# Attention rows by pairs, long beside short, and results stored two rows at a time, in a hybrid pooling and stick-breaking trunk

## The reference

```
h = rms_norm(x) ; proj = h @ w_in
u_pool, z_pool, q, k, v, z_attn, gate_logits = split(proj)
y_pool = multiscale_pool(u_pool) * silu(z_pool)
# 8 heads of 64: strictly causal, no softmax
beta  = sigmoid(q.k / 8)
A[t,s] = beta[t,s] * prod_{s<j<t} (1 - beta[t,j])
y_attn = (A @ v) * silu(z_attn)
gates = sigmoid(gate_logits + b_gate)
merged = gates0 * (y_pool @ w_pool_up) + gates1 * (y_attn @ w_attn_up)
out = rms_norm(x + merged @ w_out)
```

## Time and profile before

| what | us |
|---|---|
| median of 3 runs | 1617.39 (1616.48 to 1621.03) |
| profiled execution, its own time | 1613.6 |
| its span, first to last instruction | 1611.6 |
| TensorE matmuls busy | 1562.7 (97%) |
| VectorE busy | 1237.0 (77%) |
| GpSimd busy | 974.6 (60%) |
| ScalarE busy | 775.5 (48%) |
| mean granted TensorE clock | 0.996 |

### The profile page before, as it was taken

The page is one execution under the profiler, slowest core; times in us unless marked ns, Lnnn a source line. Parts: engine busy times, 40 slices in busy tenths (PEclk is TensorE's granted clock), DMA queues, the critical chain, the costliest instruction groups (busy, mean ns, idle before and its releaser), DMA issues. The chain is left out here.

```text
span 1611.6 us, 24736 instructions
## 1 busy us (share of the span) xinstructions
PE 1562.7 (97%) x7934; PEld 1301.4 (81%) x7934; DVE 1237.0 (77%) x1662; ACT 775.5 (48%) x1492; POOL 974.6 (60%) x697
## 2 busy tenths in 40 slices
PE   7999999999999999999999999999999999999997
PEld 6887888788888887888877888888888787778886
DVE  6744524773889889998989978889888656677987
ACT  4412222223566666666666666666666411222342
POOL 3521102421679878887778887789876233446764
PEclk9999999999999999999999999999999999999999
DMA  7633335755434243353594432433423587764552
GB/s 251 230 126 127 137 105 183 236 165 174 118 121 113 78 114 105 105 135 97 180 317 166 143 100 83 115 99 115 118 72 114 188 271 226 245 195 153 188 187 107
DMA packets 163936, 245.78 MB, mean 153 GB/s; under 512 B 47697, under 2 KB 80977, under 8 KB 163810
## 3 DMA queue, kind: packets, MB, share of 16 engines
q1 hardware_dynamic: 163810, 244.20, 48.2%
HBM read 158.15 MB, written 85.99 MB: 151 GB/s over the span
## 5 line engine op out<-in xcount | busy, mean ns | idle before, releaser
L1576 DVE TENSOR_TENSOR_SCAN left<-keep,left 128x512 f32<-128x512 f32 x192 | 296.9, 1546 | 32.0 <-issue 19.9
L1403 PE MATMUL psum<-hT,ring 128*128 128x512 f32 x644 | 264.3, 410 | 4.5 <-DVE sum_d L1612 2.4
L1643 POOL TENSOR_TENSOR ring<-raw,ring 128x512 fp32r<-128x512 f32 x138 | 231.1, 1675 | 55.2 <-ACT ring L1483 40.2
L1407 PE MATMUL psum<-hT,ring 128*128 128x512 f32 x644 | 262.8, 408 | 0.0
L1405 PE MATMUL psum<-hT,ring 128*128 128x512 f32 x644 | 262.4, 407 | 0.0
L1489 ACT ACTIVATE keep<-psum 128x512 f32<-128x512 f32 (+3 forms) x320 | 170.5, 533 | 177.5 <-PE psum L1429 175.6
L1496 ACT ACTIVATE wt<-psum 128x512 fp32r<-128x512 f32 (+3 forms) x320 | 170.9, 534 | 110.1 <-PE psum L1437 107.2
L1449 PEld LDWEIGHTS psum<-wt,vm 128*128 128x128 f32 x1088 | 170.6, 188 | 32.7 <-issue 7.0
L1582 DVE TENSOR_TENSOR wt<-psum,wt 128x512 fp32r<-128x512 f32 (+3 forms) x320 | 189.7, 593 | 7.8 <-ACT wt L1496 5.2
L1449 PE MATMUL psum<-wt,vm 128*128 128x256 f32 x1088 | 181.6, 281 | 5.1 <-DVE row_sum L1591 4.3
L1437 PE MATMUL psum<-ident,left 128*128 128x128 f32 x1088 | 170.9, 272 | 1.4 <-DVE wt L1582 1.2
(11 more groups left out here) (217 smaller groups left out, 3387.4 us busy)
## 6 DMA issues: line engine op xcount, KB each, us to landing
raw<-in_w_strips SPq DMA_DIRECT2D x92, 256.0 KB, 3.9
qm<-qk_scratch SPq DMA_DIRECT2D x128, 128.0 KB, 4.2
gate<-gate_scratch SPq DMA_DIRECT2D x64, 256.0 KB, 4.5
hT<-form_scratch SPq DMA_DIRECT2D x28, 512.0 KB, 8.3
xt<-in_x SPq DMA_DIRECT2D x16, 512.0 KB, 4.9
xT<-in_x_T SPq DMA_DIRECT2D x16, 512.0 KB, 3.8
qk_scratch<-staging SPq DMA_DIRECT2D x32, 256.0 KB, 2.6
qk_scratch<-store_lo SPq DMA_DIRECT2D x32, 256.0 KB, 3.4
```

The lines of the kernel that those rows point to most:

```text
L1403: pe.matmul(o, hi, m_hi, start=k == 0, stop=False)
L1407: last = pe.matmul(o, lo, m_hi, start=False, stop=k == HK - 1)
L1576: dve.tensor_tensor_scan(left[:, n % LN, span][:, ::-1], k, k, carry, ALU.mult, ALU.bypass).then_inc(scanned, 1)
L1643: pool.tensor_tensor(out_, a, b, op).then_inc(s, 1)
```

## The change

Rows are taken by pairs in the order of `QUERY_ORDER` = 7, 0, 6, 5, 2, 4, 3, 1 in every pass: rows 15, 14, 1, 0, 13, 12, 11, 10, 5, 4, 9, 8, 7, 6, 3, 2. Items, query units and the steps of all loads follow from this order; the planner is the same and is applied to the new list. A y_out buffer now holds 256 columns, two rows, and each pair of rows is stored by itself; the waits for the buffers, the count awaited ahead of the last stage's attention values (now up to the store of pair 6 in the last pass) and the last store follow. The rest of the kernel is unchanged.

```diff
--- before.py
+++ after.py
@@ -157,7 +157,7 @@
 
         for u in range(2):
             self.load_k(sp, 0, u, 0, NC - 1 - u)
-            self.load_q(sp, 0, u, 0, TT // 2 - 1 - u)
+            self.load_q(sp, 0, u, 0, QUERY_ORDER[u])
         for u in range(2, NC):
             self.load_k(sp, 0, u, 0, NC - 1 - u)
 
@@ -999,11 +999,15 @@
             pe.wait_ge(lo_done, STRIPS + 1)
             pe.wait_ge(staged_lo, qk_order[STRIPS - 1, 0] + 1)
             strip_product(pe, psum[:, 0, :], w_hi[:, 0, :, :], w_lo[:, 0, :, :], hT, 1)
+QUERY_ORDER = (7, 0, 6, 5, 2, 4, 3, 1)
+
+
 def attention_items():
 
 
+    rows = [i for r in QUERY_ORDER for i in (2 * r + 1, 2 * r)]
     return [(e, i, c, (i % 4 + 1) * P if c == i // 4 else CH, c == i // 4, c == 0)
-            for e in range(2) for i in reversed(range(TT)) for c in reversed(range(i // 4 + 1))]
+            for e in range(2) for i in rows for c in reversed(range(i // 4 + 1))]
 
 
 def stage3(nc, sem, psum, sb, sb_raw, ring_at, ident, bcol, v_ends, hT, w_hi, w_lo, w_strips, mix_t, mix_d, yp_d, za_d,
@@ -1129,7 +1133,7 @@
 
     KN, VN, QN = HeadLoads.KN, HeadLoads.VN, HeadLoads.QN
     kv_units = [(e, c) for e in range(2) for c in reversed(range(NC))]
-    q_units = [(e, r) for e in range(2) for r in reversed(range(TT // 2))]
+    q_units = [(e, r) for e in range(2) for r in QUERY_ORDER]
     NK, NQ = len(kv_units), len(q_units)
 
     def key_items(u):
@@ -1155,7 +1159,7 @@
 
     def query_unit(n):
         e, i = item(n)[0:2]
-        return n // NI * NQ + TT // 2 * (e + 1) - 1 - i // 2
+        return n // NI * NQ + q_units.index((e, i // 2))
 
     def at(steps, s):
 
@@ -1183,7 +1187,7 @@
     wt = sb("wt", [P, WN, 4, 2, P], F32R)
     half_sum = sb("half_sum", [P, 2 * P])
     row_sum = sb("row_sum", [P, 2, 2 * P])
-    y_out = sb("y_out", [P, 2, CH])
+    y_out = sb("y_out", [P, 2, 2 * P])
     floor = sb("floor", [P, CH])
     raws = [{b: sb_raw(f"raw{i}_{b}", [P, HK, P]) for b in (A11, A12, S3, A22)} for i in range(2)]
     second = sb("second", [P, HK, P])
@@ -1234,7 +1238,8 @@
         g, o, a, c = result_out(k)
         sp.dma_start(gate_d[strip_of(g, a) - S_G, :, c * CH:(c + 1) * CH], sums[tile_index(k)]
                      ).then_inc(sum_stored[tile_index(k)], DMA)
-        sp.dma_start(at_d[PAIRS - 1, HD:P, 0:CH], y_out[HD:P, 1, :]).then_inc(y_stored[1], DMA)
+        last = 2 * P * QUERY_ORDER[-1]
+        sp.dma_start(at_d[PAIRS - 1, HD:P, last:last + 2 * P], y_out[HD:P, 1, :]).then_inc(y_stored[1], DMA)
 
     before_in_all = (4 * len(WINDOWS) + 2 * 4 * 2 * PAIRS) // 2 * DMA
     END = ALL + 10
@@ -1299,9 +1304,9 @@
 
             def store_y(n):
                 e, i = item(n)[0:2]
-                u = row_of(n) // 4
+                u = row_of(n) // 2
                 hold(y_done, row_of(n) + 1)
-                sp.dma_start(at_d[n // NI, e * HD:(e + 1) * HD, i * P:i * P + CH],
+                sp.dma_start(at_d[n // NI, e * HD:(e + 1) * HD, i * P:(i + 2) * P],
                              y_out[e * HD:(e + 1) * HD, u % 2, :]).then_inc(y_stored[u % 2], DMA)
 
             def open_stage4(s):
@@ -1317,7 +1322,7 @@
                     opening.load_z(sp, 1, tok)
                     for i in range(opening.EARLY):
                         opening.load_piece(sp, i)
-                    sp.wait_ge(y_stored[0], (PAIRS * 4 - 1) * DMA)
+                    sp.wait_ge(y_stored[0], (PAIRS * TT // 2 - 3 + QUERY_ORDER.index(6) // 2) * DMA)
                     opening.load_y(sp, 1, tok)
 
             for s in range(-2, END):
@@ -1351,7 +1356,7 @@
                     if s == RESULT[k] + 1:
                         store_result(k)
                 for n in LAST[:-1]:
-                    if item(n)[1] % 4 == 0 and s == n + AV_LAG + 4:
+                    if item(n)[1] % 2 == 0 and s == n + AV_LAG + 4:
                         store_y(n)
 
         @block.tensor
@@ -1677,11 +1682,11 @@
             def finish_row(n):
                 e, i, row = item(n)[0], item(n)[1], row_of(n)
                 mine = slice(e * HD, e * HD + HD)
-                u = row // 4
+                u = row // 2
                 pool.wait_ge(row_done, row + 1)
-                if i % 4 == 3:
+                if i % 2 == 1:
                     wait(pool, y_stored[u % 2], u // 2, DMA)
-                step(y_out[mine, u % 2, i % 4 * P:i % 4 * P + P], row_sum[mine, row % 2, 0:P],
+                step(y_out[mine, u % 2, i % 2 * P:i % 2 * P + P], row_sum[mine, row % 2, 0:P],
                      row_sum[mine, row % 2, P:2 * P], ALU.add, y_done, row + 1)
 
             def value_diff(u):
@@ -1961,7 +1966,7 @@
                     for s, count in zip(sum_stored, SUM_STORES):
                         sp.wait_ge(s, count * DMA)
                     for s in y_stored:
-                        sp.wait_ge(s, PAIRS * 4 * DMA)
+                        sp.wait_ge(s, PAIRS * TT // 2 * DMA)
                 if m == 0 and b == 1 and c + 1 < NC:
                     sp.wait_ge(up_done, at_up(c, 1, 0))
                     opening.load_y(sp, 0, tokens(c + 1))
```

## The result

The changed kernel took 1656.27 us, the median of 5 runs (1654.46 to 1658.34), against 1617.37 us for the kernel before on the same chip (5 runs, 1614.49 to 1621.03). The ratio is 1.0251, 95% interval 1.0233 to 1.027: 38.9 us slower. The forecast was slower, 1631.0, with a range to 1645, so the sign was right and the size was not. The profiled execution took 1655.26 us, its span is 1653.3 (before 1611.6), its mean granted clock 0.985 (before 0.996).

A forecast was written before the change was run, and what follows sets the result against it. TensorE, busy 842.0 of 856 us in the attention stage, was taken as the bound. The terms 16.9 + 3.6 + 1.0 + 1.0 - 4.3 - 4.6 = +13.6 us, put on 1617.39, gave 1631.0; range 1619 to 1645.

The forecast's parts named there:

- three stalls for the value part: Starts of passes 2, 3 and 4: TensorE waits for GpSimd's late low value part, 16.9 us in sum; forecast's mechanism, 76%.
- clock behind them: After the three stalls TensorE runs at half clock for a while: +3.6 us, bounds 0 and 5.1.
- passes 5 to 8, value part: Starts of passes 5 to 8: value part possibly late, 1.0 us at the fifth and 1.0 for the other three.
- row sums: Pass ends: rows end less crowded, so TensorE's three waits for a row's sum go, -4.3 us.
- query load: Into pass 5: the first query load goes out earlier, saving its wait, -3.0 us, and -1.6 for the clock.
- key loads: Last key units get fewer steps between load and use; cost put at 0, hidden behind the items between.
- VectorE's slack: Attention stage: VectorE busy 753.6 of 856 us, taken to cover the two one-item rows behind pair 7, cost 0.
- stores: SyncE's queue and y_out's buffers: twice as many stores, half the size, cost 0, bounds 0 and 6 us.
- tie: Into pass 6: value part ends between 952.5 and 953.4, TensorE's product at 953.39; bound 1.5 us.
- Rival D: Holds or buffer waits for stores delay loads or row results at seven boundaries, adding 32 us, up to 1663; 6%.
- the lone pair: Pair 1, 0 behind pair 7: two one-item rows in a run, cost 0; otherwise a 1.4 us wait per pass.
- 1 us less per stall: GpSimd, sharing SBUF interfaces with VectorE, speeds up when VectorE lacks work; three would make +10.6 us, 1628.0.

The follow-up runs named there:

- e4: Kernel before, with only chunk 0's values loaded and split two steps later; 1640.86 us, ratio 1.0148.
- e5: Kernel before, with all value units but the first pass's loaded and split at the changed kernel's steps; 1647.3 us, ratio 1.0196.
- e8: Changed kernel with a second raw value buffer and row order 7, 0, 6, 5, 4, 3, 2, 1; 1618.78 us, ratio 1.0015.
- e1: Changed kernel with the old row order restored, each pair still stored by itself; 1639.22 us, ratio 1.0147.
- e9: e8 with the weight blocks' loads four steps later; 1619.85 us, ratio 1.0021.
- e11: e8 with two form loads in a step in place of one; 1621.1 us, ratio 1.0035.
- e6: Old row order, each pair stored by itself, with three y_out buffers in place of two; 1615.93 us, ratio 1.0004.

## Why the prediction was wrong

The mechanism of the three stalls was right, and this part of the sum. By its own steps:

| step | predicted, us | shown |
|---|---|---|
| three stalls for the value part | 6.2 + 5.0 + 5.7 = 16.9 | 5.39 + 4.77 + 5.39 = 15.6 |
| clock behind them | 3.6 | stretches at 0.5 in the whole stage: +6.7 to +9.0 |
| passes 5 to 8, value part | 2.0 | 0.34, 2.21, 1.24 at passes 5 to 7, none at 8: 3.8 |
| row sums | -4.3 | -3.7 |
| query load | -3.0 and -1.6 | -3.0; its stretch at the lower clock is gone too, and is counted in the clock's row |
| key loads | 0 | +11.3 |
| VectorE's slack | 0 | +6.5 (turns 5.5, product 1.0) |
| form load and parts' sums | none | +1.0 and -1.8 |
| stores | 0 | no wait of TensorE traced to them; GpSimd waited 0.9 for one |

With +6.7 for the clock the column comes to 36.4 us, and the stage grew by 36.1.

*Values.* The first three boundaries hold to within 1.0 us each, and e4 shows that the two steps alone make them: 17.1 us of waits in the old order. The 15.6 us are a little less than the 16.9 of the sum; 0.3 us of that at the first boundary is that join, ring part and form took 1.26 us each (1.28, 1.49 and 1.29 in rows 5). At the boundary into pass 6 the "tie" was 2.2 us, over the 1.5 that one boundary could take; the three together, 3.45, lay within the bound of 4.5.

*The step that failed* is the sentence "I cost this at 0, hidden behind the items in between" on the key loads, with the one it rests on under the stores, "nothing it loads has under three steps of room". I counted room in steps of the program. But the value chain was moved, and with it its hold, in SyncE's queue of one order: GpSimd's late part (done at 852.22) held SyncE until 852.31, and the last key load of the head stood behind. The prediction followed the late value part through GpSimd's queue and not through this one. The three steps of room for the last key unit were spent in the hold, and the landing beside the form loads took up to 9.8 us in place of the 4.2 of rows 9, so there had been no room to spare even before (0.2 us). The room itself was misread for chunk 2: its key load stood 12 steps early before, by the limit `SOON`, and not 15. Rival D had the place right (SyncE's holds making a key load late) but blamed the stores' holds, priced 4.6 us at each of seven boundaries, and got 6%. What came is one wait of 9.8 us, the most of the 11.3 that the score waited, with 10.2 us at the lower clock from inside it on, for another hold. e5 shows that it comes with the value steps alone.

*The second* is the lone pair, "at 0, covered by VectorE's slack there". A stage mean of 753.6 us in 856 says nothing of the step at which the parts' results fall. By e8 the lone pair, with the rest of the change, leaves 3.4 us, and the larger cost, about 4.5 us, is pair 2's place. The prediction priced nothing for it and misread where it goes: it says that row pairs 2 and 3 come late, but pair 2 moves forward, from items 32 to 35 of a pass to 24 to 27, and its short rows meet VectorE's 1.7 us additions in pass 3.

*The third* is the clock: one stretch was reckoned for each of three stalls. There were six stretches; what was mis-sized is the number of waits that bring one, and the length behind the longest.

*Stores.* No cost of theirs shows, but "it is idle most of the time", said of SyncE, is not why. In the old order the same stores cost 22.8 us (e1), through the buffer's turn, whose bound I gave as 6 us, from the landing of 3.1 us alone. The bound left out that GpSimd's burst and the value part stand behind the waiting row result.

*From waits to time.* In e4 the vm waits of 17.1 us cost 24.4 us, that is 1.4 us for a microsecond of wait. The 16.9 of the prediction would be 24 by that ratio, where I had 20.5. The profiled runs, 27.1 us apart, say what stands beside these waits: in the stage of e4 TensorE was idle 20.4 us more than before, 3.3 of it outside the vm waits (2.6 for products that waited for VectorE), and busy 8.2 us more, with 23.9 us at the lower clock where it was 3.4.

*GpSimd beside VectorE.* By the Trainium skill ("GPSIMD Engine Reference", "Specifications"), GpSimd shares its SBUF interfaces with VectorE, and the prediction drew 1 us less per stall from it. The trace agrees in kind: from 531.1 to 536.0 VectorE was busy 0.34 us of 4.90 and GpSimd's 512-column operations took 1.26 us each, while from 521.8 to 529.7, with VectorE at 6.74 of 7.90, they took 1.77, 2.32, 1.29 and 2.10. In sum it gave little: the three stalls came out 1.3 us under the sum, where the estimate had 3, and the operations that I had priced (1.28, 1.49 and 1.29) were already near 1.26.

**What stays open.** Whether a kernel in e8's order can gain once its form wait is gone (e9 and e11 did not get there); how pair 2's 4.5 us divide between VectorE and the loads; why GpSimd's work ahead of the hold is later and longer in the new order than in e5; and what the 3.4 us are that e8 still loses (its interval is 1.0 to 1.0031). No version ran faster than the kernel before: e6 is equal to it.

## What to carry to other kernels

When a load or an operation moves to a later step, list what stands behind it in every in-order queue it passes, holds included: here the price of a value part two steps late was 24 us, and moving the whole value chain, whose hold stands in the loading queue, made it 32, with a wait of 7.0 us through a key load that had three steps of room on paper. Give a chain of loads a second buffer before changing the order that it follows (31.0 of 38.9 us here), and a small result a third one when rows end close together. Read slack at the step in question, not as a mean over the stage, and count a wait of TensorE at more than its length.

## What the runs showed that was not expected

- A 128 KB load that lands in 4.0 us at the median took 7.0 to 9.8 us at the two key loads around pass 5; the DMA share was 0.79 and 0.87 in the 10 us behind their issues.
- Waits of one length did not cost one price. Two of 2.2 us (ending at 703.22 and 893.90) had 3.4 us at a granted clock of 0.53 behind them; two others of 2.2 us (950.73 and 994.08) had none, the clock was 1.00 in the 3.4 us behind both. What tells them apart was not tried.
- Halving the size of 32 stores and doubling their number changed the time by 0.04%, with an interval of 0.28% (e6).
